# The Fourier stage of a mixed-attention kernel: bias tables on one queue, two halves of channels, outputs copied four tiles at once

## The reference, cut to what matters

```
ug = u.reshape(B, L, 4, 64)                       # 4 groups of 64 channels
f  = fft2(ug, axes=(positions, channels)).real    # ortho norm
four = f.reshape(B, L, 256) @ w_four
```

## Time and profile before

| | |
|---|---|
| median of 3 runs | 4434.85 us |
| the profiled execution | 4439.17 us, of which the span is 4437.2 us |
| TensorE busy | 4005.8 us (90%), granted clock 0.946 |
| Fourier block, layer 0 | 788.0 to the start of the next block at 905.7 |
| Fourier block, layer 1 | 2199.2 to 2312.3 |

### The profile page before, as it was taken

One profiled execution on the slowest core, in us unless ns is written; L12 is line 12 of the kernel. 1 busy time (PEld: TensorE's weight loads), 2 busy tenths in 40 slices (PEclk: granted clock), 3 DMA queues, 4 the chain that ended last, 5 costly groups with the idle time before them and its releaser, 6 DMA issues. The chain is left out here.

```text
span 4437.2 us, 65943 instructions
## 1 busy us (share of the span) xinstructions
PE 4005.8 (90%) x24975; PEld 3247.9 (73%) x24975; DVE 2081.6 (47%) x4641; ACT 1434.7 (32%) x3276; POOL 627.7 (14%) x717
## 2 busy tenths in 40 slices
PE   7999999799669799999979858889999979979799
PEld 4777789577558688778857657767777857758687
DVE  5364111167566542111127576632760456657554
ACT  5001344156322310144317522421111467731211
POOL 3021000123020210000032210021440000000100
PEclk8999999899789899999989979989999989989899
DMA  5243221631246422222262325441221133357221
GB/s 192 88 155 134 79 76 62 221 127 57 101 169 223 177 101 72 95 75 77 110 190 102 108 84 204 176 151 68 75 76 67 46 117 109 98 192 265 81 81 62
DMA packets 224044, 525.86 MB, mean 119 GB/s; under 512 B 42830, under 2 KB 93474, under 8 KB 214386
## 3 DMA queue, kind: packets, MB, share of 16 engines
q1 hardware_dynamic: 198578, 439.01, 28.3%
q0 software_dynamic: 25152, 82.64, 5.1%
HBM read 330.43 MB, written 191.13 MB: 118 GB/s over the span
## 5 line engine op out<-in xcount | busy, mean ns | idle before, releaser
L72 PE MATMUL tm_tacc<-tm_tw_hi,hT_hi 128*128 128x384 f32 (+1 forms) x1120 | 414.4, 370 | 17.8 <-DVE tm_tw_lo L906 9.8
L73 PE MATMUL tm_tacc<-tm_tw_lo,hT_hi 128*128 128x384 f32 (+1 forms) x1120 | 410.0, 366 | 0.0
L74 PE MATMUL tm_tacc<-tm_tw_hi,hT_lo 128*128 128x384 f32 (+1 forms) x1120 | 409.9, 366 | 0.0
L72 PE MATMUL tz_tacc<-tz_tw_hi,hT_hi 128*128 128x512 f32 x896 | 359.2, 401 | 5.8 <-POOL tz_tw_lo L935 3.8
L72 PE MATMUL cm_acc<-hT_hi,cm_wb_hi 128*128 128x512 f32 (+1 forms) x912 | 363.0, 398 | 0.0
L73 PE MATMUL tz_tacc<-tz_tw_lo,hT_hi 128*128 128x512 f32 x896 | 354.7, 396 | 0.0
L74 PE MATMUL tz_tacc<-tz_tw_hi,hT_lo 128*128 128x512 f32 x896 | 354.7, 396 | 0.0
L73 PE MATMUL cm_acc<-hT_lo,cm_wb_hi 128*128 128x512 f32 (+1 forms) x912 | 344.8, 378 | 0.0
L74 PE MATMUL cm_acc<-hT_hi,cm_wb_lo 128*128 128x512 f32 (+1 forms) x912 | 344.7, 378 | 0.0
L788 DVE SCALAR_TENSOR_TENSOR tm_ds<-tm_dg,tm_ds 128x512 f32<-128x512 f32 (+1 forms) x40 | 25.6, 639 | 533.6 <-ACT tm_ds L782 533.6
L72 PEld LDWEIGHTS tm_tacc<-tm_tw_hi,hT_hi 128*128 128x128 f32 x1120 | 210.6, 188 | 60.4 <-DVE tm_tw_lo L906 14.2
(11 more groups left out here) (386 smaller groups left out, 8741.7 us busy)
## 6 DMA issues: line engine op xcount, KB each, us to landing
scr_z<-tz_tz SPq DMA_DIRECT2D x112, 256.0 KB
scr_zcm<-cm_zo SPq DMA_DIRECT2D x96, 256.0 KB, 2.0
scr_ztm<-tm_tz SPq DMA_DIRECT2D x68, 256.0 KB, 2.0
scr_xres<-out_x POOLq DMA_DIRECT2D x34, 512.0 KB, 4.1
cm_area<-in_w_ada POOLq DMA_DIRECT2D x64, 256.0 KB, 3.0
scr_z<-out_xn POOLq DMA_DIRECT2D x32, 512.0 KB, 4.8
mo_z<-scr_z SPq DMA_DIRECT2D x16, 1024.0 KB, 5.0
tz_traw<-in_w_in SPq DMA_DIRECT2D x7, 2048.0 KB, 8.5
```

What stands on the lines that cost most here:

```text
L72: nc.tensor.matmul(out, ah, bh, start=start, stop=False)
L73: nc.tensor.matmul(out, ah, bl, start=False, stop=False)
L74: return nc.tensor.matmul(out, al, bh, start=False, stop=stop)
```

## The change

The padded bias goes to POOL's queue: `load_bias` and all 48 `near` DMAs are issued by POOL. SP keeps the lines, queries and keys, which follow its first loads without a wait between.

Each direction is done in two halves of 128 channels. `w2` is laid out so that half h has its 128 real and 128 imaginary columns side by side. The first direction makes 8 PSUM banks per half, each of two t with 128 real and 128 imaginary columns (16 banks, 16 copies, 16 stores as before). After store 9, SP loads half 0 back (`load_y(0)`), and half 1 after the last store. Each load is four DMAs of runs of 1 KB.

The second direction fills a PSUM bank with four tiles of one half (8 banks); DVE copies one bank at once into `fo`, now one tile of 16 x 256, never used twice. The stores to `mix` wait for the second half and are issued by SP (odd n) and POOL (even n). The two context tiles share one bank and one copy, into `yo[0]`.

```
 SP:
-                na.load_bias(sp, l, io)
                 na.load_lines(sp, io)
                 na.load_tokens(sp, io)
-                for r in range(QR // 2): na.load_near(sp, io, r)
-                for t in range(N2): ... store yo
-                wait all y_out; 4 loads of ab
+                def load_y(h):
+                    sp.wait_ge(y_mm, NY * (h + 1))
+                    for j in range(4):
+                        sp.wait_ge(y_out[j], 32 * (h + 1))
+                    for j in range(4):
+                        sp.dma_start(ab[:, 4 * j:4 * j + 4, 256 * h:256 * h + 256], yload[h, ...]).then_inc(yi_in[h][j], 16)
+                for i in range(2 * NY):
+                    sp.wait_ge(y_ev, i + 1)
+                    sp.dma_start(ystore[i // NY, :, i % NY, :], yo[i % 4][:, :]).then_inc(y_out[i % 4], 16)
+                    if i == NY + 1:
+                        load_y(0)
+                load_y(1)
+                for n in range(1, NX, 2):
+                    sp.wait_ge(o_ev, first + 5 + n // 4)
+                    sp.dma_start(mix[n, :, :, :], fo[:, n, :]).then_inc(na.four_sp, 16)
 POOL:
-                for r in range(QR // 2, QR):
+                na.load_bias(pool, l, io)
+                for r in range(QR):
                     na.load_near(pool, io, r)
                 ...
+                for n in range(0, NX, 2):
+                    pool.wait_ge(o_ev, first + 5 + n // 4)
+                    pool.dma_start(mix[n, :, :, :], fo[:, n, :]).then_inc(na.four_pool, 16)
 TensorE, first direction:
+                for i in range(2 * NY):
+                    h, u = i // NY, i % NY
+                    if i >= 2:
+                        pe.wait_ge(y_ev, i - 1)
+                    for x in range(2):
+                        t = 2 * u + x          # four matmuls of 128 columns for each t
 TensorE, second direction:
+                for j in range(8):
+                    h, b = j // 4, ready(first + j)
+                    pe.wait_ge(yi_in[h][j % 4], 16)
+                    for x in range(4):         # two matmuls of 128 columns for each of four tiles
 DVE:
+                for j in range(8):
+                    dve.wait_ge(o_mm, i + 1)
+                    nc.vector.tensor_copy(fo[:, 4 * (j % 4):4 * (j % 4) + 4, 128 * h:128 * h + 128], acc[i % 2] as 4 x 128)
```

More of the change, by code:

```diff
@@ L1027, in __init__ @@
         self.lines_in, self.mask_ok, self.table_ok = P.sem("lines_in"), P.sem("mask_ok"), P.sem("table_ok")
-        self.near_pool = P.sem("near_pool")
-        self.four_out = [P.sem(f"four_out{j}") for j in range(6)]
+        self.four_sp, self.four_pool = P.sem("four_sp"), P.sem("four_pool")
     def four_stored(self, eng):
-        tiles = NX if self.last else NT
-        for j, sem in enumerate(self.four_out):
-            eng.wait_ge(sem, 16 * ((tiles + 5 - j) // 6))
+        eng.wait_ge(self.four_sp, 16 * (NX // 2))
+        eng.wait_ge(self.four_pool, 16 * (NX // 2 if self.last else NT - NX // 2))
     def load_bias(self, eng, l, io):
@@ L1120, in fourier_phase @@
         dc = P.sb("dc", [128, 2, 2, 256])
+        NAB = N2 if na.last else N2 + 2
+        LF = LX if na.last else LT
         ab = P.sb("ab", [128, N2 + 2, 512])
         yo = [P.sb(f"yo{j}", [128, 512]) for j in range(4)]
-        NF = len(na.four_out)
-        fo = [P.sb(f"fo{j}", [128, 256]) for j in range(NF)]
+        fo = P.sb("fo", [128, NX, 256])
         acc = [P.ps(f"acc{b}") for b in range(6)]
@@ L1129, in fourier_phase @@
         y_out = [P.sem(f"y_out{j}") for j in range(4)]
[L1130 to L1135, removed]
+        yi_in = [[P.sem(f"yi_in{h}{j}") for j in range(4)] for h in range(2)]
+        NY = N2 // 2
+        ystore = io["four_y"].rearrange("(h p u) c -> h p u c", h=2, u=NY)
+        yload = io["four_y"].rearrange("(h r) (x c) -> h (r x) c", h=2, x=2)
+        first = 0 if na.last else 1
+        NO = first + 8
+        mix = io["mix"][0:LX, 0:256].rearrange("(a b c) d -> b a c d", a=16, b=16)
         with nc.Block() as block:
@@ L1196, in channels, with ready @@
                     last.then_inc(ab_mm, 1)
+                def ready(i):
+                    if i >= 2:
+                        pe.wait_ge(o_ev, i - 1)
+                    return acc[i % 2]
                 for t in range(N2):
@@ L1211, in _ @@
-                for t in range(N2, NAB):
-                    channels(t)
-                pe.wait_ge(d2_in, 32)
[L1214 to L1225, removed]
+                for i in range(2 * NY):
+                    h, u = i // NY, i % NY
+                    if i >= 2:
+                        pe.wait_ge(y_ev, i - 1)
+                    for x in range(2):
+                        t = 2 * u + x
+                        re, im = ab[:, t, 256 * h:256 * h + 128], ab[:, t, 256 * h + 128:256 * h + 256]
+                        b = acc[4 + i % 2][:, 256 * x:256 * x + 256]
+                        nc.tensor.matmul(b[:, 0:128], d1[:, t, 0, :], re, start=True, stop=False)
+                        nc.tensor.matmul(b[:, 0:128], d1[:, t, 2, :], im, start=False, stop=True)
+                        nc.tensor.matmul(b[:, 128:256], d1[:, t, 1, :], re, start=True, stop=False)
+                        last = nc.tensor.matmul(b[:, 128:256], d1[:, t, 0, :], im, start=False, stop=True)
+                    last.then_inc(y_mm, 1)
@@ L1226, in _ @@
+                pe.wait_ge(d2_in, 32)
+                if first:
+                    for t in range(N2, NAB):
+                        channels(t)
+                    b = ready(0)
+                    pe.wait_ge(ab_dve, NAB // 2)
+                    pe.wait_ge(ab_act, NAB // 2)
+                    for n in range(2):
                         for k in range(2):
+                            both = ab[:, N2 + k, :].rearrange("p (h s c) -> p s h c", h=2, s=2)
                             for cs in range(2):
-                                last = nc.tensor.matmul(b[:, 0:256], dc[:, cs, k, (n - 16) * 128:(n - 15) * 128],
-                                                        ab[:, N2 + k, cs * 256:(cs + 1) * 256],
-                                                        start=(k + cs == 0), stop=(k + cs == 2))
+                                last = nc.tensor.matmul(b[:, 256 * n:256 * n + 256], dc[:, cs, k, n * 128:(n + 1) * 128],
+                                                        both[:, cs, :, :], start=(k + cs == 0), stop=(k + cs == 2))
+                    last.then_inc(o_mm, 1)
@@ new lines, in _ @@
+                for j in range(8):
+                    h, b = j // 4, ready(first + j)
+                    pe.wait_ge(yi_in[h][j % 4], 16)
+                    for x in range(4):
+                        n = 4 * (j % 4) + x
+                        nc.tensor.matmul(b[:, 128 * x:128 * x + 128], d2[:, 0, :], ab[:, n, 256 * h:256 * h + 128], start=True, stop=False)
+                        last = nc.tensor.matmul(b[:, 128 * x:128 * x + 128], d2[:, 1, :], ab[:, n, 256 * h + 128:256 * h + 256], start=False, stop=True)
```

67 lines of the change are left out of this document (25 added, 42 removed).

## The result

Medians: 4435.87 us before (4 runs, 4430.83 to 4438.4) and 4408.59 us after (4 runs, 4404.08 to 4410.31); ratio 0.9938 [0.9921, 0.9956]. The change is 27 us faster. The profiled execution of the changed kernel took 4407.12 us, its span 4405.3 us (clock 0.949), which is 31.9 us under the span of before.

A forecast was written before the change was run, and what follows sets the result against it. TensorE's holes in the Fourier blocks were taken as the bound: late-issued stores in the first direction and layer 1's turn between directions. Gains of 14.8 us (layer 0) and 18.1 (layer 1), together 33, gave 4402 us, range 4391 to 4420.

The forecast's parts named there:

- `fx`: Block start: POOL's `pad` chain shares the DMA engines with the first loads, costing 1.3 us a layer (0 to 3).
- hole: First direction: TensorE stands still 14.1 us (layer 0) and 12.4 us (layer 1) because stores are issued late.
- store 10: First direction: it stands behind the 2 MB of `load_y(0)`, costing 1 us a layer (0 to 3).
- second direction: Last first-direction matmul to last store issue: gains 3.2 us in layer 0, 8.2 us in layer 1.
- Bias to POOL's queue: First direction: stores issue once copies finish; gains 14.7 us (layer 0), 13.0 us (layer 1), leaving 2 and 1 us waiting.
- The keys' landing: Layer 0, queue ahead of the first-direction stores: queries and keys, issued at about 795, land at 836 to 841.
- `near` on one queue: Layer 0: POOL's 48 loads start at about 801, land by about 847 (843 to 857), before DVE is needed; cost 0.
- 128-column passes: First direction: twice as many passes, 0.111 us each instead of 0.216, costing 0.8 us a layer.
- rival B: Both directions: weight loads bound the halved passes at 0.19 us each; 27 us slower, 4462 us; chance 0.04.
- A: First direction: 48 `near` loads delay the keys to near 850, leaving about 11 us standstill per layer; 4420 us; chance 0.12.
- C: Block outputs: `near` lands so late that DVE holds them up, 21 us later in layer 0; 4475 us; chance 0.04.
- the prediction's signs: Fourier blocks: ScalarE's store waits under 5 us, full clock through the first direction, spans near 103 and 95 us.

The follow-up runs named there:

- bias alone: Kernel before with only the padded bias and all 48 `near` loads moved to POOL's queue; 4418.56 us, ratio 0.9969.
- halves alone: Changed kernel with the bias loads put back (`load_bias` and 24 `near` on SP, 24 on POOL); 4426.47 us, ratio 0.9985.
- late keys: Changed kernel with the keys loaded by SP after `load_y(1)` instead of ahead of the first-direction stores, both layers; 4403.07 us, ratio 0.9931.
- stores off POOL: Changed kernel with POOL's half of the output stores and the two context stores issued by ScalarE; 4396.99 us, ratio 0.9912; again 4398.79, 0.9913.
- one store queue: Changed kernel with all 16 output stores to `mix` issued by POOL, none by SP; 4411.7 us, ratio 0.9943.

## Why the prediction was right

The time, the direction and the main mechanism came out as forecast: 4408.6 for 4402, in a range of 4391 to 4420. The terms, forecast and measured, by the stages of the table above:

| | layer 0 forecast | measured | layer 1 forecast | measured |
|---|---|---|---|---|
| first loads (`fx`), to the first copy | −1.3 | −2.5 | −1.3 | −3.0 |
| first direction: hole, passes, store 10 | +12.9 | +11.1 | +11.2 | +11.7 |
| second direction to the last issue | +3.2 | +4.4 | +8.2 | +10.4 |
| end of the block | 0 | −1.4 | 0 | −1.6 |
| sum | 14.8 | 11.6 | 18.1 | 17.6 |

*Bias to POOL's queue.* Right, with a remainder that was too small: 2 us of the hole were to stay in layer 0 and 1 in layer 1; TensorE waited 2.6 and 0.7 (2.6 to 3.0 and 0.7 to 2.6 over three profiles of the change). Sixteen banks at 1.787 us would take 27.4 from the first copy's start to the last one's end; layer 0 took 32.4. So 5.0 us are lost there, for 3 that the forecast gave to the keys and to store 10. By copy 8 4.5 are gone, with the lower clock behind the short wait (0.63 over 4 us), which this term of the sum left out; store 10 adds 0.6. The bias alone and the halves alone show that this part owns the hole.

*The keys' landing.* Partly luck. 836 to 841 was forecast for a block that starts at 788, so 48 to 53 us into it; 840.6 was measured in a block that starts at 786.05, so 54.6 (51.0 in layer 1). The forecast's own figures, 811 and 24 to 26 more, give 835 to 837 and not up to 841. And the way there was another: SP was to issue the keys at 795, but it stood 11.77 us in one small issue, with nothing to wait for in the program, and issued them at 805.64. In the kernel before, SP stood 35.51 us in 24 issues, which the prediction did put down to the queue; it did not ask when the first loads alone would hold an issue up. Whether that cost anything was not tested; what lies ahead in the queue may set the landing whenever the issue comes. Late keys took the wait away in each of three blocks, so what stays of the hole is theirs.

*`near` on one queue.* Forecast from 801 to 847; issued from 802.52, and DVE's wait ended at 844.68. The cover held. POOL's second step took 11.5 us to land beside the loads; alone it was taken as 4.3 us, and the forecast start already allowed for more.

*`fx`.* The wait was of the right size: 2.34 and 2.11 us, of which 1.38 were there before, so 1.0 and 0.7 for a forecast of 1.3 (which by the prediction's own rates would have been 1.0 to 1.1). It does not come every time: in layer 1 of the two further profiles of the change it is absent. What was left out is the clock behind it, 1.5 us more in the channels of each layer. The first copy came at 42.8 to 45.6 in layer 0 over three profiles of the change.

*128-column passes.* Right. Copies 1.787 us apart for 16 passes are 0.112 each, for a forecast of 0.111, and rival B would have needed 0.154.

*The second direction.* Better than forecast by 1.2 and 2.2 us. The wait before the second half was 0.9 us in place of 2.3, and the clock did not fall.

*The end of the block.* This step is missing from the prediction. It took the issue of the last stores as the end and the rest as equal. The drain of POOL's queue behind it grew from 3.9 to 5.6 us in layer 1 with more transfers on that queue, and would have been visible in the profile before as the 4.3 us between the last store and the next block.

*Rivals.* A would have left 11 us of each hole; 5.6 and 3.5 us of waits were left in ScalarE and less on TensorE. C needed `near` to land at 876; it landed at 844.6. Two of the prediction's signs failed by a little: ScalarE's waits in layer 0 were 5.6 us and not under 5, and the clock was not full through the first direction.

The error of 6.6 us on the median is −2.9 for the start with `fx` and its clock, −3.0 for the ends, −1.3 for the first direction and +3.4 for the second, −3.8 in all, and the runs' own spread: the three profiles of the change have blocks of 198.0 to 202.2 us in all, the median of before moved from 4434.85 to 4435.87 with one more run, and the two further medians of the change are 4402.61 and 4405.64.

## What to carry to other kernels

A store that waits is often late by what stands ahead of it in the same queue: follow it back to its issue, and from there to what its issuing engine waited for. Once that is moved, ask again what is ahead, and what the work now does beside its new neighbours: one of the experiments here removed a wait and got it back at the block's end, and another removed one without any gain in the time. Before an experiment's profile is read as its effect, look whether the difference begins ahead of the edit. Read the end of a block as closely as its middle, and let the engine that issues its last transfers be one whose drain is short.

## What the runs showed of the hardware

POOL's drain at a block's end is the landing of its own last transfer and a rest behind it. The rest goes with the number of transfers that POOL has issued in the block, and not with how late the last one lands. Layer 1, us; the landing is that of POOL's last DMA, from the drain's start:

| run | transfers on POOL's queue | to the last landing | rest | drain |
|---|---|---|---|---|
| halves alone | 32 | 2.92 | 1.37 | 4.29 |
| before | 40 | 2.18 | 1.72 | 3.90 |
| stores off POOL (drain in the middle of the block) | 50 | 15.14 | 2.09 | 17.24 |
| after | 58 | 3.15 | 2.43 | 5.58 |
| late keys | 58 | 6.88 | 2.42 | 9.30 |
| bias alone | 66 | 2.18 | 3.68 | 5.86 |
| one store queue | 66 | 3.53 | 3.42 | 6.95 |

From 32 to 58 transfers the rest grows by about 0.04 us for each (an estimate from these rows), and by 1.0 to 1.3 more to 66; layer 0, with two more transfers in most of these runs, shows the same steps (1.45 at 34, 2.5 at 60, 3.6 to 3.9 at 68). Why, the runs do not tell. The late keys lengthen the landing alone, the bias alone the rest alone. SP drained in 0.37 us and ScalarE in 0.42 with eight stores each just issued and not yet landed.

An engine can stand for long inside a single DMA issue: SP did for 11.77 us in layer 0 and 9.60 in layer 1, at an issue of 32 KB for which the program has no wait, with 7 MB of its own loads just issued ahead of it on the same queue. In the kernel before, the same small loads came after the first loads had landed and took 0.6 to 0.8 us each. That the queue was full is the likely reason; no run shows it.
